# First mixer fed with the input before its norm factor, and decay exponents formed in two signed halves

## The reference

```python
def rms_norm(x, g):
    y = x * lax.rsqrt(jnp.mean(x * x, axis=-1, keepdims=True) + EPS)
    return y * g

def gla_mixer(h, w_in, w_gk_up, b_gk, g_onorm, w_out):      # h = rms_norm(x, norm_mix)
    proj = h @ w_in
    q, k, v, r, gk_low = split(proj)                        # widths 512, 512, 1024, 1024, 16
    log_a = log_sigmoid(gk_low @ w_gk_up + b_gk) / 16
    # per head, chunks of 64 tokens:
    b = cumsum(log_a)                                       # within a chunk, never rising
    decay = exp(where(causal, b_i - b_j, -inf))
    attn = einsum('ik,jk,ijk->ij', q, k, decay)
    ...                                                     # state carried from chunk to chunk
    o = rms_norm(o, g_onorm)
    return (o * silu(r)) @ w_out
```

## Time and profile before

| | |
|---|---|
| median of three runs | 1641.07 us (1639.46 to 1641.47) |
| profiled execution | 1639.36 us, of which 1637.5 us are the span from its first to its last instruction |
| TensorE busy | 1583.8 us, 97% of the span |
| VectorE, ScalarE, GpSimd busy | 1128.2, 799.9 and 222.3 us |
| mean granted TensorE clock | 0.991 of full |

### The profile page before, as it was taken

The page is one execution under the profiler, slowest core; times in us unless marked ns, Lnnn a source line. Parts: engine busy times, 40 slices in busy tenths (PEclk is TensorE's granted clock), DMA queues, the critical chain, the costliest instruction groups (busy, mean ns, idle before and its releaser), DMA issues.

```text
span 1637.5 us, 24024 instructions
## 1 busy us (share of the span) xinstructions
PE 1583.8 (97%) x9298; PEld 1267.7 (77%) x9298; DVE 1128.2 (69%) x1709; ACT 799.9 (49%) x1230; POOL 222.3 (14%) x206
## 2 busy tenths in 40 slices
PE   6999989999999999999999999999999999999999
PEld 3777767888888887667667887878888888888887
DVE  5555544595959597788676758576685468686868
ACT  6455553644444456334554435363463373636353
POOL 0233340000000001233310501305031000000000
PEclk8999999999999999999999999999999999999999
DMA  4222212524241412223203123121320361414131
GB/s 149 78 65 66 78 39 77 193 66 139 62 144 57 143 33 84 65 64 90 54 1 103 53 67 89 41 78 41 82 73 14 93 204 64 141 65 141 65 103 52
DMA packets 197856, 135.85 MB, mean 83 GB/s; under 512 B 10667, under 2 KB 185276, under 8 KB 197748
## 3 DMA queue, kind: packets, MB, share of 16 engines
q1 hardware_dynamic: 197748, 134.36, 27.4%
HBM read 132.16 MB, written 2.18 MB: 82 GB/s over the span
## 4 chain that ended last, share of the span: by engine, by line
PE 78%; DVE 9%; issue 7%; ACT 4%; POOL 1%; DMA 1%; SPq 0%; PEldq 0%; ACTq 0%; POOLq 0%; DVEq 0%; PEld 0%
PE bank L241 11%; PE bank L243 11%; PE bank L242 11%; PE bank L997 6%; PE bank L998 6%; PE bank L999 6%; PE bank L505 4%; PE bank L2004 4%; PE bank L507 3%; PE bank L506 3%; DVE arena L2308 2%; DVE w_lo L225 1%; ACT w_hi L221 1%; PE bank L1829 1%; PE bank L1558 1%
## 5 line engine op out<-in xcount | busy, mean ns | idle before, releaser
L225 DVE TENSOR_TENSOR w_lo<-raw,w_hi 128x1024 fp32r<-128x1024 f32 x154 | 192.9, 1253 | 97.7 <-ACT w_hi L221 97.1
L241 PE MATMUL bank<-m_hi,w_hi 128*128 128x512 f32 x592 | 233.8, 395 | 4.4 <-POOL w_lo L231 2.8
L243 PE MATMUL bank<-m_hi,w_lo 128*128 128x512 f32 x592 | 230.7, 390 | 0.0
L242 PE MATMUL bank<-m_lo,w_hi 128*128 128x512 f32 x592 | 230.5, 389 | 0.0
L221 ACT CAST w_hi<-raw 128x1024 fp32r<-128x1024 f32 x170 | 177.5, 1044 | 87.7 <-PE bank L243 55.4
L1029 ACT CAST d_hi<-arena 128x1024 fp32r<-128x1024 f32 x112 | 117.9, 1053 | 130.7 <-PE bank L999 130.7
L241 PE MATMUL bank<-h_hi,w_hi 128*128 128x512 f32 x368 | 148.0, 402 | 9.0 <-DVE h_lo L376 4.7
L243 PE MATMUL bank<-h_hi,w_lo 128*128 128x512 f32 x368 | 145.3, 395 | 0.0
L242 PE MATMUL bank<-h_lo,w_hi 128*128 128x512 f32 x368 | 145.2, 395 | 0.0
L1034 DVE TENSOR_TENSOR d_lo<-arena,d_hi 128x1024 fp32r<-128x1024 f32 x112 | 136.1, 1220 | 10.9 <-ACT d_hi L1029 10.8
L241 PEld LDWEIGHTS bank<-m_hi,w_hi 128*128 128x128 f32 x592 | 111.1, 188 | 30.6 <-POOL w_lo L231 3.2
(11 more groups left out here) (327 smaller groups left out, 3332.8 us busy)
## 6 DMA issues: line engine op xcount, KB each, us to landing
raw<-in_w_in SPq DMA_DIRECT2D x64, 512.0 KB, 3.8
raw<-in_l_w_ff SPq DMA_DIRECT2D x32, 512.0 KB, 4.1
arena<-in_l_w_ff SPq DMA_DIRECT2D x32, 512.0 KB, 5.7
raw<-in_w_mlp_up SPq DMA_DIRECT2D x32, 512.0 KB, 4.1
arena<-in_w_mlp_down SPq DMA_DIRECT2D x32, 512.0 KB, 5.5
raw<-in_l_w_in SPq DMA_DIRECT2D x24, 512.0 KB, 3.8
raw<-in_l_w_out SPq DMA_DIRECT2D x8, 512.0 KB, 4.1
arena<-gb_rows SPq DMA_DIRECT2D x16, 256.0 KB, 4.9
```

Of the source, the lines that this page charges most:

```text
L225: dve.tensor_tensor(w_lo[q.par][:], raw[q.par][:], w_hi[q.par][:].bitcast(F32), ALU.subtract).then_inc(s["w_ready"], 1)
L241: pe.matmul(g_bank[q.par][:], w_hi[q.par][:, k], hi[:, k], start=(k == 0), stop=False)
L242: pe.matmul(g_bank[q.par][:], w_hi[q.par][:, k], lo[:, k], start=False, stop=False)
L243: last = pe.matmul(g_bank[q.par][:], w_lo[q.par][:, k], hi[:, k], start=False, stop=(k == KT - 1))
```

## The change

The high and low parts are taken of gain times x, without the factor, straight from the transposition's bank, so the first products start before the sum of squares is known. The squares are summed over each token's row in the layout that x arrives in; the factor is formed as a column, turned by four small products, and multiplied into results where they are read: into the 16 gate rows, and into q, k, v and the gate panels as VectorE empties their banks. ScalarE empties none of these banks any more; tanh is taken from the scaled copy. The gate panel shrinks to its 16 columns, and its eight products, q's and k's are spread over the opening. The gates' work is reordered by heads. The first barrier becomes a count without a wait. The differences of a level are formed in two instructions, one for each half of a block, in the order that makes each negative; the absolute value goes, and the division by 16 is the exponential's scale. Two transfers move: constants behind the second panel, the last norm's gain to the first MLP.

```diff
         def sp_start(sp):
...
+            sp.dma_start(ident[:], const_square[:, 0:P]).then_inc(s["x_in"], 16)
+            x_piece(0)
+            gain(*gain_rows[0], "mix_in")
+            load(sp, Panel(N_GK, 0, 0, 0), [(rows(t["l0_w_in"])[:, :, GLA_G0:GLA_G0 + GLA_RANK], 0)])
+            x_piece(1)
+            x_piece(2)
+            load(sp, N_Q0, [(rows(t["l0_w_in"])[:, :, GLA_Q0:GLA_Q0 + P], 0)])
+            x_piece(3)
+            for row in gain_rows[1:]:
+                gain(*row, "params_in")
...
+        def pe_rank(pe, k):
...
+            pe.wait_ge(s["h_ready"], k + 1)
+            o = g_bank[q.par][0:GLA_RANK, :]
+            left, left_lo = w_hi[q.par][:, k, 0:GLA_RANK], w_lo[q.par][:, k, 0:GLA_RANK]
+            pe.matmul(o, left, h_hi[:, k], start=(k == 0), stop=False)
+            pe.matmul(o, left, h_lo[:, k], start=False, stop=False)
+            last = pe.matmul(o, left_lo, h_hi[:, k], start=False, stop=(k == KT - 1))
...
         def pe_start(pe):
...
+            turn(0)
+            pe.wait_ge(s["mix_in"], 16)
+            pe.transpose(b[5][:, 0:KT], par_rows[0:KT, 0, :], ident[0:KT, 0:KT]).then_inc(s["par_t"], 1)
+            for k in range(1, 4):
+                turn(k)
+            pe_rank(pe, 0)
+            pe_rank(pe, 1)
+            turn(4)
+            turn(5)
+            for k in range(2, 6):
+                pe_rank(pe, k)
+            turn(6)
+            turn(7)
+            for k in range(4):
+                pe_eighth(pe, N_Q0, k)
+            pe_rank(pe, 6)
+            pe_rank(pe, 7)
+            for k in range(4, KT):
+                pe_eighth(pe, N_Q0, k)
             pe.wait_ge(s["params_in"], 16 * PARAM_DMAS)
...
         def act_start(act):
...
+            def high(k):
                 act.wait_ge(s["x_t"], k + 1)
+                act.activation(h_hi[:, k], b[k % 6][:], ACT.Copy, scale=gains[:, k:k + 1]).then_inc(s["n_hi"], 1)
+
+            def squares(j, tt):
+                c = slice(j * SEQ, (j + 1) * SEQ)
+                act.activation(x_junk[:, tt, c], x_tok[:, tt, c], ACT.Square, accum_out=sq_cols[:, j, tt:tt + 1]
+                               ).then_inc(s["n_sq"], 1)
...
+            for k in range(4):
+                high(k)
+            act.wait_ge(s["x_in1"], 16)
+            for tt in range(TT):
+                squares(0, tt)
+            high(4)
+            high(5)
+            act_split(act, N_Q0)
+            high(6)
+            high(7)
+            act.wait_ge(s["x_in3"], 16)
+            squares(1, 0)
+            squares(1, 1)
+            act_split(act, N_Q0.next())
+            squares(1, 2)
+            squares(1, 3)
+            keep_x(4)
+            act.wait_ge(s["n_t"], 1)
...
+            act_split(act, Panel(N_GLA, 12, 0, 2))
+            for k in range(5, KT):
+                keep_x(k)
+            act.wait_ge(s["n_ss"], 1)
+            act.copy(r_0, b[4][:]).then_inc(s["n_r0"], 1)
...
         def dve_start(dve):
...
             def low(k):
                 dve.wait_ge(s["n_hi"], k + 1)
-                dve.tensor_tensor(h_lo[:, k], hb[:, k % 2], h_hi[:, k].bitcast(F32), ALU.subtract).then_inc(s["h_ready"], 1)
+                dve.scalar_tensor_tensor(h_lo[:, k], b[k % 6][:], gains[:, k:k + 1], h_hi[:, k].bitcast(F32),
+                                         ALU.mult, ALU.subtract).then_inc(s["h_ready"], 1)
...
+            low(0)
+            low(1)
+            keep_x(0)
+            keep_x(1)
+            low(2)
+            low(3)
+            keep_x(2)
+            keep_x(3)
+            low(4)
+            low(5)
+            dve_split(dve, N_Q0)
+            low(6)
+            low(7)
+            dve_split(dve, N_Q0.next())
...
+        def dve_gates(dve, evac, exponent):
...
+            dve.wait_ge(s["n_r0"], 1)
+            dve.tensor_tensor(gk_low[0:GLA_RANK, :], gk_low[0:GLA_RANK, :], r_0[0:GLA_RANK, :], ALU.mult).then_inc(s["gkl"], 1)
+            evac(0, 0, 0, N_Q0)
+            dve.wait_ge(s["gk_in"], 32)
+            least(0)
+            least(1)
+            sums(0)
+            evac(0, 0, 1, Panel(N_GLA, 12, 0, 1))
+            dve_split(dve, Panel(N_GLA, 12, 0, 3))
+            sums(1)
+            dve.wait_ge(s["gscan"], 2)
+            exponent(0, 0)
+            exponent(0, 1)
+            evac(0, 0, 2, Panel(N_GLA, 12, 0, 2))
+            dve_split(dve, Panel(N_GLA, 12, 0, 4))
+            least(2)
+            least(3)
+            sums(2)
+            sums(3)
+            evac(0, 0, 3, Panel(N_GLA, 12, 0, 3))
...
         def act_gla(act):
...
+            def gate(g, e, u):
+                act.wait_ge(s["z_in"], 2 * g + u - 3)
+                act.activation(tgate[:, u - 4], head_in[e][:, u], ACT.Tanh, scale=0.5).then_inc(s["tg"], 1)
...
                 act.wait_ge(s["arg_r"], NL * g + i + 1)
-                act.activation(arg[:, i % 2], arg[:, i % 2], ACT.Abs).then_inc(s["ab_r"], 1)
...
-                act.activation(ex[:, i % 2], arg[:, i % 2], ACT.Exp, scale=-1.0).then_inc(s["ex_r"], 1)
+                act.activation(ex[:, i % 2], arg[:, i % 2], ACT.Exp, scale=1.0 / GLA_GATE_NORM).then_inc(s["ex_r"], 1)
...
         def dve_gla(dve):
             def evac(g, e, u, q):
...
+                else:
+                    dve.tensor_tensor(dst, g_bank[q.par][:], r_0, ALU.mult).then_inc(s["z_in"], 1)
+                    dve.wait_ge(s["z_in"], 2 * g + u - 3)
+                dve.sem_inc(bank_free[q.par], 1)
+
+            def gated(g, e, u):
+                dst = head_in[e][:, u]
+                dve.wait_ge(s["tg"], 2 * g + u - 3)
+                dve.scalar_tensor_tensor(dst, tgate[:, u - 4], 1.0, dst, ALU.add, ALU.mult).then_inc(s["zg"], 1)
...
-                dve.tensor_tensor(arg[:, i % 2].rearrange("p (c t) -> p c t", t=w), v,
-                                  v[:, :, c:c + 1].broadcast_to([P, SEQ // w, w]), ALU.subtract).then_inc(s["arg_r"], 1)
+                a, m = arg[:, i % 2].rearrange("p (c t) -> p c t", t=w), c + 1
+                last = dve.tensor_tensor(a[:, :, 0:m], v[:, :, c:m].broadcast_to([P, SEQ // w, m]), v[:, :, 0:m], ALU.subtract)
+                if m < w:
+                    last = dve.tensor_tensor(a[:, :, m:w], v[:, :, m:w], v[:, :, c:m].broadcast_to([P, SEQ // w, w - m]),
+                                             ALU.subtract)
+                last.then_inc(s["arg_r"], 1)
...
                     if lv == 1 or lv == 3:
                         evac(h, e, 4 + lv // 2, q(4 + lv // 2))
+                    if lv == 2 or lv == 4:
+                        gated(h, e, 3 + lv // 2)
+                    if lv == 5 and front:
+                        evac(h + 1, e + 1, 0, q(6))
                 if front:
+                    evac(h + 1, e + 1, 1, q(7))
                     dve_split(dve, q(9))
...
                 if g == 0:
                     sp.wait_ge(s["phase_done"], 8 * (i + 1))
+                    if i == 0 and hf == 0:
+                        sp.dma_start(g_rep[:], t["final_norm"].rearrange("(o d) -> o d", o=1).broadcast_to([P, D])
...
-            pe_norm(pe)
-            pe.wait_ge(s["memsets"], 3)
-            fence(pe, 1)
+            pe.sem_inc(s["phase_done"], 1)
             pe_gates(pe)
```

More of the change, by code:

```diff
@@ L397, in build @@
+            dve_split(dve, Panel(N_GLA, 12, 0, 2))
+        def pe_norm(pe):
+            pe.wait_ge(s["n_bc"], 1)
+            pe.wait_ge(s["x_a"], 1)
+            for tt in range(TT):
+                last = pe.matmul(b[4][:, tt * P:(tt + 1) * P], r_wide[:, tt * P:(tt + 1) * P], ident[:], start=True, stop=True)
+            last.then_inc(s["n_ss"], 1)
         at[0] = keep_at = 6 * SEQ
@@ L437, in sp_gla @@
                 for u, c in enumerate(starts):
-                    load(sp, Panel(N_GLA, 6, h, u), [(w[:, :, bass.ds(c, P)], 0)])
-        def pe_gates(pe):
-            pe_panel(pe, Panel(N_GK, 0, 0, 0), h_hi, h_lo, s["h_ready"], 0)
+                    if u >= first:
+                        load(sp, Panel(N_GLA, 6, h, u), [(w[:, :, bass.ds(c, P)], 0)])
+                    if first and u == 1:
+                        sp_consts(sp)
+            head(0, 1)
+            with sp.Fori(1, GLA_H) as h:
+                head(h, 0)
+        def pe_gates(pe):
+            q = N_Q0.next()
+            pe_eighth(pe, q, 0)
+            pe_eighth(pe, q, 1)
+            pe_norm(pe)
+            for k in range(2, 6):
+                pe_eighth(pe, q, k)
             pe.wait_ge(s["gk_in"], 32)
-            pe.wait_ge(s["gkl"], 1)
+            pe.wait_ge(s["gkl"], 2)
+            pe.wait_ge(s["par_s"], 3)
+            pe.wait_ge(s["x_a"], 4)
             for h in range(GLA_H):
@@ L474, in dve_gates, with sums @@
                                   ALU.add, ALU.min).then_inc(s["gm"], 1)
-            dve_split(dve, Panel(N_GLA, 12, 0, 1))
-            for h in range(GLA_H):
+            def sums(h):
                 dve.wait_ge(s["gm"], h + 1)
@@ L524, in pe_gla @@
         def pe_gla(pe):
-            for u in range(4):
+            for u in (2, 3):
```

245 lines of the change are left out of this document (109 added, 136 removed).

## The result

The kernel before took 1641.27 us in the median of four runs, the changed one 1622.76; the ratio is 0.9885, 95% interval 0.9863 to 0.9906. The forecast was 1620 (1613 to 1629.5): it held, and so did its sign.

What follows compares the result with a forecast made beforehand. TensorE, busy 97% of the span, was taken to bound the kernel. Gains of 16.9 (opening), 0 (first three heads) and 3 us (last head) took 1639.36 to 1619.5, or 1621 by the median; forecast 1620, range 1613 to 1629.5.

Steps and rivals of the forecast that it cites:

- The opening, 16.9 us: From x landing to head 0's first block product: head 0 starts at 49.0 instead of 65.9 us, gaining 16.9 (11 to 20).
- The clock in the opening, 3.0 us: Loss from TensorE at half clock, added to a full-clock schedule with head 0 at 46.0; ends 0 and 6.9 us.
- Triples 4 and 5: Fifth and sixth of the gate's eight rank-16 product triples in the opening, forecast to be through at 17.0 us.
- the wait that I had listed ahead of them: TensorE waits over a microsecond for k=4's low part, out at 15.5 us, because ScalarE has four squares (3.1 us) first.
- VectorE's cover of 1.3 us: Second v panel released at 49.4 us, wanted by TensorE in head 0 at 50.7; any VectorE loss beyond 1.3 is paid.
- Heads 1 and 2 at nothing: In the first three heads VectorE gets 3.5 us more each, hidden in some 20 us of its pauses: worth 0.
- The rival that VectorE holds the heads: VectorE's added work makes block products wait 1.5 to 3 us in each of four heads; about 1629 us, chance 0.10.
- The last head, 3 us: Fourth head: without the absolute value the decay chain TensorE waits for is shorter; gain 3 us, bounds 1 and 5.
- The wait that was to fall under 1 us: TensorE's wait at the last head's sixth level, 2.65 us before the change, forecast to be under 1 us.
- The contention: VectorE and GpSimd hold each other up: the last head's two gate products take back up to 1.4 us, giving 1621.
- What else moves, at nothing: Last norm's 512 KB gain moved ahead of the MLP's first down-projection weights: costs nothing; GpSimd's removed barrier costs nothing.
- Sum: Opening 16.9, first three heads 0 and last head 3 add up to a gain of 19.9 us.

Runs made afterwards that it cites:

- e6_scans_later: Changed kernel with the gate scans of heads 2 and 3 moved from ahead of head 0 to the end of head 0's levels; 1621.76 us.
- e1_abs_back: Changed kernel with the one-instruction exponent on VectorE and ScalarE's absolute value put back, the new opening kept; 1628.83 us.
- e8_last_gates: Changed kernel with, in the last head, the sixth exponent ahead of the weight split and two gate products behind the last level; 1621.53 us.
- e5_warm: Changed kernel with nine products of a constant tile added on TensorE ahead of the first transposition; 1621.59 us.

## Why the prediction held, point by point

- **The opening, 16.9 us: right.** Head 0 at 49.0 was forecast and 48.67 measured; at full clock 46.0 against 45.4 to 45.6. On the way: up-projection at 30.1 (29.5, and 31.0 in the execution shown above), the q panel's end at 24.7 (25.3 above). The 64 KB of narrow columns had to be there at 7.2; their price came elsewhere, as 1.15 us of wait for the second piece of x at 8.58 us behind them, which I had not listed. Some of the gain is clock: from 14.7 us on TensorE was busy at the 1.2 GHz level for 13.2 us of the old opening (in 16.96 to 27.20, 37.44 to 40.85 and 54.50 to 57.92) and for 3.4 us of the new one, and half of such time is lost: by this estimate up to 5 of the 17.2 us are clock. What the single parts of the new opening bring (the factor behind the products, the barrier gone, the order of the transfers) was not taken apart.
- **The clock in the opening, 3.0 us: taken high, and of a size that nothing here foretells.** In twelve profiled executions with the new opening, the stretch behind the up-projection ran at half clock for 0 us (six), 3.4 us (four) or 6.8 us (two), which costs 0, 1.7 or 3.4, 1.1 on average. That the execution shown came so near to 49.0 is in part luck: it is one with 3.4 us at half clock. The full clock that I assumed from 10 us on wasn't there either: the first two triples took 1.43 and 1.28 us instead of 0.69. Triples 4 and 5 were through at 17.4 all the same, where I had 17.0, since the wait that I had listed ahead of them did not show in that execution.
- **VectorE's cover of 1.3 us: gone, as named.** The 1.3 us were reckoned for a head 0 at 46.0; for the 49.0 that I forecast they would have been 4.3 with the same times on VectorE. The v panel was forecast out at 49.4 and was at 53.4, since scans of 1.22 us took 2.20 and 1.76 beside GpSimd. The panel was just in time (TensorE transposed the v tiles from 53.50 on), but VectorE entered the levels late, and that cost 1.2 us of head 0 (e6_scans_later).
- **Heads 1 and 2 at nothing: right sum, wrong reason.** The added work isn't hidden by VectorE's pauses: the shorter decay chain pays for it. It is also more than I took: 6.4 us in head 1 (26.8 to 33.3) and not 3.5. The rival that VectorE holds the heads, at 1.5 to 3 us each, is what happens without the signed halves (1.2 and 1.8 us, e1_abs_back).
- **The last head, 3 us: the step that failed.** It lost 1.4. I had followed the chain forward with a pair 0.10 us dearer, and it was 0.50 on average; with a gate product of 0.69, and it was 1.22; and I had not put the split's wait for ScalarE ahead of the sixth exponent. The wait that was to fall under 1 us became 2.94. TensorE's waits in this head add up to 3.3 us before (0.29, 0.37, 2.65) and after (2.94, 0.39), so what the shorter chain saved went to the factor's work (e1_abs_back); the loss is clock, 6.8 us at the lower level behind the long wait instead of 3.4 (1.7 us). With the order mended the head takes 35.64 us, 2.5 less than before the change (e8_last_gates); whether that order would have won as much with the absolute value still in the chain was not tested.
- **The contention was named and taken at too little.** Rows first: one gate product takes 1.22 us beside GpSimd, two take 1.29 behind it. The Trainium skill (SBUF — State Buffer, section "SBUF: two separate sides") states that a VectorE instruction with two SBUF inputs and a GpSimd instruction that reads SBUF exclude each other for the whole instruction. The trace agrees in kind, with the durations above. By that rule I gave 1.4 us for the two gate products, but the halved exponents, the scans and the gates' differences read two SBUF inputs too and were stretched as well.
- **What else moves, at nothing: right.** From the MLP on nothing changed, 512 KB of gain included.
- **Range.** Its lower end, 1613, is named as full clock with a gain of 25; 1641.07 − 25 is 1616. The measured time lies within it either way.
- **Sum.** 17.2 − 1.2 + 0.4 − 1.4 = 15.0 us in the two traces, against 16.9 + 0 + 3 = 19.9; the spans differ by 15.4. So the heads lost 2.2 us where the forecast had them win 3. The medians differ by 18.5, since the trace before is of a short execution (1639.36 us) and the one after of a long one (1624.12); executions of the changed kernel alone differ by 5 us with the granted clock (last section).
- **Which half did it.** By the medians of one chip: the opening with the absolute value left in 13.3 us (1642.10 to 1628.83), the signed halves on top of it 6.4, of which the heads show 3.8.

## What to carry to other kernels

Take the two halves of a change apart even when the total comes out as forecast: here the new place of a factor cost the heads what the shorter chain gave them, and neither shows in the sum. On an engine that works in order, ask for every instruction that feeds a chain what stands ahead of it, and whether that waits for another engine. Cost VectorE's work from SBUF at its duration beside GpSimd wherever GpSimd is at work, and a pause of TensorE with the slow stretch behind it.

## What the runs showed of the hardware

- The spread of one kernel is the clock. In twelve executions of the changed kernel the span follows the mean granted clock: 0.996 gives 1617.4 to 1617.8 us, 0.995 1619.5 to 1620.1, 0.994 1620.8 to 1622.1, 0.993 1622.5 to 1622.8. These 0.003 of clock are worth 5 us, more than any small term of the sum, so edits of 1 us are read from the trace, not from medians. The kernel before ran at 0.986 to 0.992: part of the gain of the opening is clock that was granted.
- In the opening the column of the granted clock says 1.00 from 10.2 to 12.9 us, while products of 512 columns follow each other at 0.43 us there and at 0.23 from 14.9 on. So in these first microseconds the pitch shows the lower level, and the column does not; with products ahead of x (e5_warm) they came at 0.23 from 8.8 us on.
